# Pool and convolution-gate panels of a hybrid decoder block as seven products, with weight sums made in DRAM

## The reference, cut to what matters

```python
h = rmsnorm(x, g_mix)
proj = h @ w_in
za, zb, zc, zg = jnp.split(proj, IN_SPLITS, axis=-1)
ya = chunked_spatial_gating(gelu(za), ...) @ w_branch_a
yb = short_gated_conv(zb, b_conv) @ w_branch_b     # gb, gc, xin = split(zb); gb * conv3(gc * xin)
yc = multiscale_pool(zc, c_wg, c_scale) @ w_branch_c
gates = sigmoid(zg + b_gate)                        # three gates of 1024 columns
merged = gates[0] * ya + gates[1] * yb + gates[2] * yc
x = x + merged @ w_o
```

## Time and profile before

| what | value |
|---|---|
| median of 3 runs | 884.42 us (884.3 to 884.81) |
| the profiled execution's own time | 884.56 us |
| its span | 882.7 us |
| PE busy, share of the span | 874.2 us, 99% |
| DVE, ACT, POOL busy | 649.0, 420.0, 78.4 us |
| load of a weight panel, from issue to landing (median of 68) | 4.8 us |
| a step of POOL's loop: copy, accumulate, accumulate | 1024, 768, 512 KB |

### The profile page before, as it was taken

One profiled execution on the slowest core, in us unless ns is written; L12 is line 12 of the kernel. 1 busy time (PEld: TensorE's weight loads), 2 busy tenths in 40 slices (PEclk: granted clock), 3 DMA queues, 4 the chain that ended last, 5 costly groups with the idle time before them and its releaser, 6 DMA issues.

```text
span 882.7 us, 13301 instructions
## 1 busy us (share of the span) xinstructions
PE 874.2 (99%) x5232; PEld 781.9 (89%) x5232; DVE 649.0 (74%) x825; ACT 420.0 (48%) x629; POOL 78.4 (9%) x89
## 2 busy tenths in 40 slices
PE   9999999999999999999999999999999999999997
PEld 7998888889999999988888888899999999988885
DVE  5684667688676687765456465898888888789877
ACT  6655432345444544533234332455554455467555
POOL 0101011112110000014200045000000000000001
PEclk9999999999999999999999999999999999999999
DMA  9956449999987423472221123214222332376522
GB/s 341 371 186 237 145 176 223 261 212 288 244 217 180 143 78 114 144 333 97 96 96 48 48 68 123 96 49 141 97 95 95 101 123 97 107 242 236 191 95 96
DMA packets 26012, 139.64 MB, mean 158 GB/s; under 512 B 2800, under 2 KB 2928, under 8 KB 13936
## 3 DMA queue, kind: packets, MB, share of 16 engines
q1 hardware_dynamic: 17728, 101.85, 32.1%
q0 software_dynamic: 6064, 25.17, 12.6%
q10 hardware_dynamic: 2176, 12.00, 3.6%
HBM read 132.72 MB, written 29.88 MB: 184 GB/s over the span
## 4 chain that ended last, share of the span: by engine, by line
PE 90%; DVE 5%; ACT 2%; issue 1%; DMA 1%; ACTq 0%; POOLq 0%; POOL 0%; DVEq 0%
PE psum L1614 30%; PE psum L1616 29%; PE psum L1615 29%; DMA pack<-first 1%; DVE tl L980 1%; DVE wl L980 1%; ACT wh L455 0%; DVE fol L980 0%; PE psum L1666 0%; PE psum L1866 0%; DVE w7l L980 0%; DVE hn L1401 0%; PE psum L1993 0%; DVE gt L1391 0%; ACT th L455 0%
## 5 line engine op out<-in xcount | busy, mean ns | idle before, releaser
L1614 PE MATMUL psum<-th,w7h 128*128 128x256 f32 x504 | 142.7, 283 | 0.3 <-ACT snap L455 0.3
L1615 PE MATMUL psum<-tl,w7h 128*128 128x256 f32 x504 | 142.6, 283 | 0.0
L1616 PE MATMUL psum<-th,w7l 128*128 128x256 f32 x504 | 142.6, 283 | 0.0
L980 DVE TENSOR_TENSOR wl<-raw,wh 128x2048 fp32r<-128x2048 f32 (+1 forms) x44 | 89.2, 2039 | 49.2 <-ACT wh L455 49.1
L1614 PEld LDWEIGHTS psum<-th,w7h 128*128 128x128 f32 x504 | 96.7, 192 | 0.5 <-issue 0.5
L1615 PEld LDWEIGHTS psum<-tl,w7h 128*128 128x128 f32 x504 | 96.8, 192 | 0.0
L1616 PEld LDWEIGHTS psum<-th,w7l 128*128 128x128 f32 x504 | 96.8, 192 | 0.0
L455 ACT ACTIVATE wh<-raw 128x2048 fp32r<-128x2048 f32 (+1 forms) x44 | 73.1, 1675 | 21.1 <-PE psum L1616 19.8
L1614 PE MATMUL psum<-hh,wh 128*128 128x512 f32 x192 | 75.0, 391 | 0.0
L1616 PE MATMUL psum<-hh,wl 128*128 128x512 f32 x192 | 74.7, 389 | 0.0
L1615 PE MATMUL psum<-hl,wh 128*128 128x512 f32 x192 | 74.7, 389 | 0.0
(11 more groups left out here) (280 smaller groups left out, 2282.7 us busy)
## 6 DMA issues: line engine op xcount, KB each, us to landing
raw<-weights SPq DMA_DIRECT2D x68, 1024.0 KB, 4.8
fo_sums<-fo POOLq DMA_DIRECT2D x10, 1024.0 KB, 5.9
fo_sums<-fo POOLq DMA_DIRECT2D x10, 768.0 KB, 10.3
fo_sums<-fo_sums POOLq DMA_DIRECT2D x10, 512.0 KB, 13.6
raw<-fo_sums SPq DMA_DIRECT2D x10, 512.0 KB, 4.7
more<-fo_sums SPq DMA_DIRECT2D x10, 512.0 KB, 4.7
more<-fo SPq DMA_DIRECT2D x6, 512.0 KB, 3.7
pack<-first SPq DMA_DIRECT2D x3, 768.0 KB, 8.2
```

Of the source, the lines that this page charges most:

```text
L980: return V.tensor_tensor(dst, v, f32(hi), ALU.subtract)
L1614: nc.tensor.matmul(dst, lh, rh, start=start, stop=False, **kw)
L1615: nc.tensor.matmul(dst, lh, rl, start=False, stop=False, **kw)
L1616: return nc.tensor.matmul(dst, ll, rh, start=False, stop=stop, **kw)
```

## The change

It does the following.

- PC0, PC0+1, GB0 and GB0+1 become panels of seven products like those of GA0. `NG`, the number of such panels, goes from 12 to 16.
- The weight sums of these four panels and of GA0 (`ND` = 5, "from the third key panel on") are not made by DVE: POOL issues 15 transfers (`together`), in ten waits, from the end of the third key panel on, that copy the panels into a DRAM tensor `w_sums` and add blocks in place. SP loads the sums into a buffer of their own (`sums`, two slots) and the rest of the panel into `raw`. The signs of the token sums are changed so that all sums are additions; the right half of a panel comes out negative, which is taken back by scales of -1.
- These four panels keep their intermediate values in `gsnap_first`, since `gsnap` overlaps tiles that are still in use there.
- For them and for the first two gate panels the products are in another order (`seven_plain_first`): the plain blocks first.
- The order of ACT and DVE between the transposes and the first branch panel is written anew. The pool's scale is applied in ACT's copy and in DVE's low part (`lo_scaled`), and four separate multiplications (L1247) go.
- POOL's loop for `fo_sums` starts after GA0+1 and not after the mixing.
- The start: `WARM` goes from 14 to 12, a step of `v_half(0)` is issued as two matmuls for each pair of operands with waits of their own (`v_step`), and `xt` is loaded in two halves.

```diff
-WARM = 14
+WARM = 12
-            sp.dma_start(xt[:], xt_in).then_inc(xt_here, 16)
+            for half in range(2):
+                ts = slice(2 * half, 2 * half + 2)
+                sp.dma_start(xt[:, ts, :], xt_in[:, ts, :]).then_inc(xt_here[half], 16)
...
+            together(("copy", 0))
+            together(("s1", 0), ("s3", 0))
+            together(("s2", 0), ("copy", 1))
             for t in range(TT):
                 pool.wait_ge(var_ready, t + 3)
                 rsqrt(small(RS + t), small(VR + t), 1).then_inc(rstd_ready, 1)
+            together(("s4", 0), ("s1", 1))
+            together(("s3", 1))
+            together(("s2", 1), ("copy", 2))
+            together(("s4", 1), ("s1", 2))
+            together(("s3", 2))
+            together(("s2", 2))
+            together(("s4", 2))
             pool.wait_ge(mixed, 4)
-            pool.dma_start(wgr[:], wg_in).then_inc(wg_here, 16)
+            pool.dma_start(wgr[:], wg_in).then_inc(wg_gf_here, 16)
...
+            def v_step(k):
+                pe.wait_ge(memh_ready, k + 1)
+                pe.wait_ge(*of_piece(k, piece_hi, hi_ready))
+                for mt in range(MT):
+                    nc.tensor.matmul(bank[6 + mt][:], memh[:, k, parts[mt]], wh[:, k // 4, cs], start=k == 0, stop=False)
+                pe.wait_ge(meml_ready, k + 1)
+                for mt in range(MT):
+                    nc.tensor.matmul(bank[6 + mt][:], meml[:, k, parts[mt]], wh[:, k // 4, cs], start=False, stop=False)
+                pe.wait_ge(*of_piece(k, piece_lo, lo_ready))
+                for mt in range(MT):
+                    ins = nc.tensor.matmul(bank[6 + mt][:], memh[:, k, parts[mt]], wl[:, k // 4, cs], start=False, stop=k == KT - 1)
...
+            def seven_plain_first(n, i, j, free):
+                left, right = bank[2 * j], bank[2 * j + 1]
+                pe.wait_ge(lo_a, i + 1)
+                pe.wait_ge(*free)
+                gate_product(right[:, Q:S], n, 0, 1, "B11", start=True).then_inc(p1_done, 1)
+                gate_product(left[:, 0:Q], n, 0, 2, "B21", start=True)
+                pe.wait_ge(s1_kept, i + 1)
+                gate_product(right[:, 0:Q], n, 0, 0, "T4")
+                pe.wait_ge(lo_s13, i + 1)
+                gate_product(left[:, Q:S], n, 1, 0, "T1").then_inc(p5_done, 1)
+                gate_product(right[:, Q:S], n, 1, 1, "T2").then_inc(p6_done, 1)
+                pe.wait_ge(lo_ready, n + 1)
+                pe.wait_ge(s5_kept, i + 1)
+                gate_product(left[:, Q:S], n, 2, 1, "B22").then_inc(p3_done, 1)
+                pe.wait_ge(u2_kept, i + 1)
+                gate_product(right[:, Q:S], n, 2, 0, "T3").then_inc(panel_done, 1)
...
             for n in range(2):
-                fm_panel(PC0 + n, h_hi, h_lo, first_tile, [(cx_ready, 2 * n + t + 1) for t in range(2)])
+                seven_plain_first(PC0 + n, n, n, (cx_ready, 2 * n + 2))
             for n in range(2):
-                fm_panel(GB0 + n, h_hi, h_lo, first_tile, [(zp_ready, 2 * n + t + 1) for t in range(2)])
+                seven_plain_first(GB0 + n, 2 + n, n, (zp_ready, 2 * n + 2))
```

More of the change, by code:

```diff
@@ L393, in _, with transfer, together @@
             rsqrt(small(RM, MT), small(VM, MT), MT).then_inc(rstd_ready, 1)
+            made = [0]
+            def transfer(dst, src, **kw):
+                made[0] += 16
+                pool.dma_start(dst, src, **kw).then_inc(sums_made, 16)
+            def together(*transfers):
+                pool.wait_ge(sums_made, made[0])
+                for part, g in transfers:
+                    two, src = w_sums[2 * g:min(2 * g + 2, ND)], weights[PC0 + 2 * g - 2:PC0 + min(2 * g + 2, ND) - 2]
+                    if part == "copy":
+                        transfer(two, src.rearrange("n p (b f) -> n p b f", b=4))
+                    elif part == "s1":
+                        transfer(two[:, :, 0, :], src[:, :, 4 * P:8 * P], accum_op=ALU.add)
+                    elif part == "s3":
+                        transfer(two[:, :, 2, :], src[:, :, 0:4 * P], accum_op=ALU.add)
+                    elif part == "s2":
+                        transfer(two[:, :, 1, :], two[:, :, 2, :], accum_op=ALU.add)
+                    else:
+                        transfer(two[:, :, 3, :], two[:, :, 1, :], accum_op=ALU.add)
             pool.wait_ge(panel_done, K0 + 1)
@@ new lines, in gate_prep_lo, with add_left @@
+            def gate_prep_lo(n, i):
+                blocks, p = sums[:, i % 2] if by_transfer(n) else raw_blocks(n % SLOTS), n % 2
+                dve.wait_ge(hi_s13, i + 1)
+                lo(gate_lo[p][1], blocks[:, 0:2], gate_hi[p][1]).then_inc(lo_s13, 1)
+                if not by_transfer(n):
+                    dve.wait_ge(s4_ready, i - ND + 1)
+                dve.wait_ge(hi_ready, n + 1)
+                lo(gate_lo[p][2], blocks[:, 2:4], gate_hi[p][2]).then_inc(lo_ready, 1)
+            def add_left(n, i, j):
+                held = gsnap_first if i < 4 else gsnap
+                dve.wait_ge(p3_done, i + 1)
+                dve.wait_ge(u2_kept, i + 1)
+                V.tensor_tensor(bank[2 * j], bank[2 * j], held[:, 0, :], ALU.add).then_inc(gate_sum, 1)
@@ L1137, in _, with add_right, gate_add @@
+            def add_right(n, i, j):
+                held = gsnap_first if i < 4 else gsnap
+                dve.wait_ge(panel_done, n + 1)
+                dve.wait_ge(u3_kept, i + 1)
+                V.tensor_tensor(bank[2 * j + 1], bank[2 * j + 1], held[:, 1, :], ALU.add).then_inc(up_sum, 1)
+            def gate_add(n, i, j):
+                add_left(n, i, j)
+                add_right(n, i, j)
             for n in range(2):
-                split_lo(XI0 + n + 1)
                 if n == 0:
+                    split_lo(XI0 + 1)
```

409 lines of the change are left out of this document (238 added, 171 removed).

## The result

The changed kernel takes **892.57 us** (median of 4 runs, 890.14 to 893.47) against 884.62 us (4 runs, 884.3 to 885.05): ratio 1.0082, 95% interval 1.007 to 1.0094. It is 8.0 us slower. The forecast was 885.1 us in a range up to 887.2, so the result lies outside it. The profiled execution took 893.43 us, span 891.7.

What follows compares the result with a forecast made beforehand. PE was taken as the bound, busy 874.2 of 882.7 us. The terms -2.96 - 0.5 - 0.33 + 3.5 + 0.75 + 0.2 = +0.66 on 884.56 gave 885.1 us against 884.42, range 881.0 to 887.2.

Steps and rivals of the forecast that it cites:

- (a): PC0 to GB0+1: four panels in seven products take 10.14 us each instead of 10.88, -2.96 us on PE.
- (c): Pool's linear map: its last matmul group no longer waits for the fourth window, -0.33 us.
- (b): Kernel start: step 1 begins 0.78 us sooner; -0.5 us taken, lower end 0.3 if the third key panel's load stays.
- (d): GB0+1: PE waits for ACT's copy "s1", behind GB0's left addition, which DVE makes after the fourth window, +3.5 us.
- (e): Ahead of the first branch panel: PE waits for convolution low parts that DVE makes last, +0.75 us (0 to 1.5).
- (f): Transfers: beside POOL's chain, 70 us long, a weight panel loads 2.2 us later; +0.2 us (0 to +2).
- the clock rival: PE's clock falls to 1.2 GHz in the wait of (d), slowing two products: +2.9 us, 888.0 us; chance 0.12.
- the rival of late sums: POOL's accumulations run slower, the ten steps end at 185 us and cost 15: 900 us; chance 0.04.

Runs made afterwards that it cites:

- late_wg: Changed kernel with POOL's chain held back until SV0+1's high part is made, and `wgr`'s load moved ahead of the chain's last two steps: 887.78 us.
- late_swap_conv_wg: late_swap_conv with `wgr`'s load moved ahead of the chain's last two steps: 881.43 us, ratio 0.996.
- b_start: Kernel before with the change's start alone (`WARM` 12, V product's first half step by step, `xt` in halves): 884.83 us.
- b_start_copy3: Kernel before with the change's start and the first three transfers of POOL's chain: 889.57 us, ratio 1.0045.
- late_swap_conv: late_swap with the four low parts of the convolution's output put ahead of the add ending the last gate panel's sum: 882.79 us.
- late_fill: Changed kernel with POOL's chain held back until SV0+1's high part is made, and 16 useless matmuls in PE's stop in GB0+1: 887.46 us.
- b_copy: Kernel before with one 2 MB copy within DRAM, issued by POOL where the change's first transfer is: 884.73 us, ratio 0.9995.
- swap: Changed kernel with DVE's add for `gate_sum` 3 put ahead of the fourth pool window: 887.8 us, ratio 1.0029.
- fill: Changed kernel with eight useless matmuls in PE's stop in GB0+1: 892.31 us, ratio 1.0072.
- swap_oldstart: swap with the start put back to that of the kernel before: 886.96 us, ratio 1.0011.
- late_swap: swap with POOL's chain also held back until SV0+1's high part is made: 884.05 us, ratio 0.9987.
- late_swap_conv_nofo: late_swap_conv with POOL's `fo_sums` loop starting right behind its first chain: 882.58 us, ratio 0.9973.

## Why the prediction was wrong, by its own steps

**(a) Four panels in seven products: right.** PE ended GB0+1's first two products at 183.01 - 3.32 = 179.69 in late_wg, where nothing had come in between; the working said 179.6. In late_swap_conv_wg, where no wait is left, the stretch from transposes to branch panel is 64.96 us long against 68.88: -3.9 where (a) and (c) give -3.3. The other 0.6 us have no step in the working.

**(b) The start: -0.5 was put down, and nothing came.** Step 1 did begin sooner, at 8.30, but SV0 began at 54.76 in place of 54.80. The wait for the third key panel's load was 2.02 us (39.01 us) instead of 1.34, since ACT came sooner and the load, at 39.01 against 38.78, did not. That is the lower end, and even its 0.3 us did not stay; b_start has 884.83 against 884.9. What the Trainium skill, "DMA: Bandwidth & Descriptors", section "Queues, rings and completion order", says of one ring in order gave the better end here. What I did not ask is what a faster PE would release: it brought POOL's copy ahead of a load. With the chain's first transfers beside it, the start costs (b_start_copy3).

**(c)** cannot be told from (a): the pool's linear map waits no more.

**(d) The new wait in GB0+1: right, +3.5 against 3.31.** With the start of the list undisturbed the copy was due at 183.1, and in late_wg PE went on at 183.01. In the changed kernel PE and DVE had both come about 5 us late by then.

**(e)** +0.75 against 1.10 us, within its bounds. The working's own terms give 13.9 - 13.05 = 0.85. Whether the wait counts in full is open: late_swap_conv took it away and moved the branch panel by 0.24 us in the profile.

**(f) Transfers: this is the step that failed.** I took +0.2, in bounds of 0 to +2, for a weight panel loaded 2.2 us later. The load of SV0+1 took 6.7 us more (11.5 against 4.8), ACT waited 3.79 us for it and PE 3.18, and the clock behind it cost 1.7 more: 4.9 us in the profile. Two things were missed. I applied a mean rate, 7.0 us per MB, to a load that meets one particular transfer: 1 MB took 11.5 us with 2 MB issued 0.67 us ahead of it, and 4.8 us, as if alone, with the same 2 MB issued 0.36 us behind it. And the bound took no account of the clock rival, which I priced for step (d) only. The chain's own length was off as well: 102 us from its first issue at 48.73 to its last at 150.82, and a landing more, for the 70 worked out; in the changed kernel the sums and `wgr` were nevertheless there in time, and the rival of late sums did not come.

**The clock** fell in the wait of (d), a rival at 0.12. It lost 1.7 us where the rival had 2.9, and late_fill shows that the stop was the cause. The Trainium skill, "TensorE: Matmul & The Clock Gate", section "HAM oscillation — how this bites in real kernels", says that gaps send the clock down and that work behind them starts at half rate; the changed kernel's trace agrees at both stops, the traces of b_copy (2.22 us) and swap (2.94 us) show stops without it, and by that rule the clock belonged into the forecast.

Set together in the profiled execution: -3.3 (a, c), +3.3 (d), +1.1 (e), +3.2 (load), +3.4 (clock, twice) make +7.7, against +7.6 at the first branch panel. The close fit is in part luck: with the -3.9 measured for (a) and (c) it is +7.1. Against the +0.66 forecast, (f) with its clock is off by 4.7 us, the clock behind (d) by 1.7, (b) by 0.5 and (e) by 0.35. Of the rest of the span, 0.8 us lie between 314 and 346 us, 0.5 of them a wait for a copy in `gsnap`, and 0.7 at the end; I did not follow these further. In two of four executions of the changed kernel (890.14, 891.71) something of this is missing; which part, a time alone does not say.

## What to carry to other kernels

A new background transfer is priced by what it meets, not by its mean rate: list the loads issued within a few us of it, on whose completion an engine hangs with little room, and ask which event releases each of the two, since here some 0.5 us of order went with about 4.8 us of time. A gain upstream is not free where it moves such a release; start it alone, the transfer alone, and both. A stop of PE like those here is costed together with the half-speed stretch behind it, and stops in a row hide one another: take them out together before you judge an idea, which here turned +8.0 into -3.8 us.

## What the runs showed of the hardware that was not expected

- **Order of issue between queues.** The same 1 MB load landed 10.4 to 11.8 us after its issue when another queue's 2 MB copy had been issued 0.14 to 0.67 us ahead of it, and after 4.8 us with the copy 0.26 or 0.36 us behind. The Trainium skill, "DMA: Bandwidth & Descriptors", section "Queues, rings and completion order", says that an engine goes round the queues that have work, a packet at a time. The rows bear this out in part: a packet of the copy holds 64 KB (2.10 MB in 32 packets), one of the load 8 KB (0.13 MB in 16), and in swap, fill and b_start_copy3 just 16 packets of the load moved between 49 and 54 us, beside the whole copy; in the changed kernel none did. Why 0.26 us behind is enough for the load to go first, no run here shows.
- **An issue can block its engine.** ACT's issue of a 1 MB write took 0.46 us before, 2.37 us in the changed kernel, 5.86 us in swap and 6.27 us in swap_oldstart.
- **The clock.** Behind stops of 2.22 (b_copy) and 2.94 us (swap) it stayed at 1.00; behind 3.18, 3.25, 3.31, 3.32, 3.39, 3.45 and 4.83 us it went to 0.50. What is missing to full speed was 1.7 us behind 3.18, 3.25, 3.31 and 3.32, and 3.4 us behind 3.39, 3.45 and 4.83 (a part of it still within the stop). Each is one trace.
- **Spread.** Where such a race is open, executions of one kernel differ by up to 6.6 us (swap_oldstart); with the copy held back, by 1.8 to 3.3 (late_swap, late_swap_conv, late_swap_conv_nofo) and by 0.6 (late_swap_conv_wg).
